# A modulation read as rows and an S5 state carried over token pairs: one change to a mixture-of-experts and state-space block in fp32

## The reference, cut to what matters

```python
cond = jax.nn.silu(c)                       # c: 1 x 1024
mod = cond @ ada_w[l] + ada_b[l]            # ada_w: 1024 x 6144
sh1, sc1, g1, sh2, sc2, g2 = jnp.split(mod, 6, axis=-1)
```

```
x[t] = a * x[t-1] + B u[t]          a = exp(lambda * step), complex, |a| < 1
y[t] = Re(C x[t]) + D * u[t]
```

## Time and profile before

| | us |
|---|---|
| median of the runs (3) | 3221.09 |
| the profiled execution | 3219.63 |
| its span in the trace | 3218.0 |
| TensorE busy | 2962.3 (92%) |
| VectorE busy | 1349.6 (42%) |
| ScalarE busy | 928.4 (29%) |

### The profile page before, as it was taken

The page is one execution under the profiler, slowest core; times in us unless marked ns, Lnnn a source line. Parts: engine busy times, 40 slices in busy tenths (PEclk is TensorE's granted clock), DMA queues, the critical chain, the costliest instruction groups (busy, mean ns, idle before and its releaser), DMA issues. The chain is left out here.

```text
span 3218.0 us, 46119 instructions
## 1 busy us (share of the span) xinstructions
PE 2962.3 (92%) x18349; PEld 2221.3 (69%) x18349; DVE 1349.6 (42%) x1820; ACT 928.4 (29%) x1160; POOL 68.1 (2%) x130
## 2 busy tenths in 40 slices
PE   8997899999999999999969999899799699999898
PEld 7886444334333333389858888899799587988897
DVE  1334311111111111154389756454544498645544
ACT  0122011111111111154222445344543222564443
POOL 3001000000000000010000000000100000000000
PEclk8958799999999999999989999999999899999899
DMA  6436499999999999985423433455565233525452
GB/s 215 144 117 233 175 418 418 417 418 418 418 418 418 417 418 418 413 243 191 128 67 105 154 112 123 151 178 169 150 219 168 73 94 104 168 98 163 155 184 79
DMA packets 343178, 737.74 MB, mean 229 GB/s; under 512 B 14200, under 2 KB 259504, under 8 KB 308224
## 3 DMA queue, kind: packets, MB, share of 16 engines
q1 hardware_dynamic: 338272, 726.71, 62.0%
q0 software_dynamic: 4768, 9.12, 1.3%
HBM read 734.73 MB, written 1.05 MB: 229 GB/s over the span
## 5 line engine op out<-in xcount | busy, mean ns | idle before, releaser
L476 PE MATMUL ps<-arena,ring 128*128 128x256 f32 x2304 | 520.3, 386 | 4.6 <-DVE arena L380 4.6
L1352 PE MATMUL ps<-u_upper,w_lower 128*128 128x256 f32 x1984 | 522.9, 284 | 0.6 <-DVEq L2191 0.5
L476 PEld LDWEIGHTS ps<-arena,ring 128*128 128x128 f32 x2304 | 440.7, 193 | 70.1 <-DVE arena L380 4.9
L1352 PE MATMUL ps<-u_upper,w_upper 128*128 128x256 f32 x1408 | 400.5, 284 | 3.5 <-DVE u_lower L1746 3.5
L1352 PE MATMUL ps<-u_lower,w_upper 128*128 128x256 f32 x1408 | 399.3, 284 | 0.0
L1740 DVE TENSOR_TENSOR w_lower<-ring,w_upper 128x2048 fp32r<-128x2048 f32 x128 | 293.3, 2292 | 215.9 <-ACT w_upper L1705 215.9
L1389 PE MATMUL ps<-arena 128*64 128x512 f32 x1632 | 365.4, 598 | 13.9 <-DMA arena<-in_exp_w_up 13.9
L1352 PEld LDWEIGHTS ps<-u_upper,w_lower 128*128 128x128 f32 x1984 | 367.7, 192 | 1.4 <-DVEq L2191 1.4
L1504 DVE TENSOR_SCALAR arena<-ps 128x512 f32<-128x512 f32 x34 | 23.5, 692 | 791.1 <-PE ps L1389 791.1
L1705 ACT ACTIVATE w_upper<-ring 128x2048 fp32r<-128x2048 f32 x128 | 244.7, 1912 | 195.8 <-PE ps L1352 195.7
L1389 PEld LDWEIGHTS ps<-arena 128*64 128x64 f32 x1632 | 110.2, 137 | 251.9 <-issue 197.6
(11 more groups left out here) (581 smaller groups left out, 3783.9 us busy)
## 6 DMA issues: line engine op xcount, KB each, us to landing
arena<-in_exp_w_up SPq DMA_DIRECT2D x204, 1024.0 KB, 20.2
ring<-in_exp_w_down SPq DMA_DIRECT2D x136, 1024.0 KB, 22.4
ring<-in_w_in SPq DMA_DIRECT2D x75, 1024.0 KB, 5.8
ring<-in_exp_w_up SPq DMA_DIRECT2D x68, 1024.0 KB, 24.1
ring<-in_ffn_w_gate SPq DMA_DIRECT2D x44, 1024.0 KB, 5.8
ring<-in_ffn_w_up SPq DMA_DIRECT2D x44, 1024.0 KB, 5.4
ring<-in_ffn_w_down SPq DMA_DIRECT2D x44, 1024.0 KB, 4.9
ring<-in_ada_w SPq DMA_DIRECT2D x24, 1024.0 KB, 5.2
```

What stands on the lines that cost most here:

```text
L476: ins = nc.tensor.matmul(bank(b, 2, TOK)[:, m, :], w[:, k, m * P:(m + 1) * P], rhs[:, k, :], start=(k == 0 and (part is None or (part == 0 ...
L1352: ins = nc.tensor.matmul(out_, w_ if w_is_lhs else x_, x_ if w_is_lhs else w_, start=start and n == 0, stop=stop and n == 2, skip_group_ch ...
```

## The change

**Modulation.** `ada_w` is read in 24 row slices of 128 x 2048, one DMA of 8 KB runs each. `mod_slice` has one column of `cond` as the stationary operand (128 x 1) and the slice as the moving one: four matmuls of 512 columns, which write to the partitions 0, 32, 64 and 96 of one bank. Eight slices give 2048 outputs, as rows. ScalarE copies four rows out of PSUM (`mod_rows_copy`), and `mod_turn` brings those that are wanted over the partitions there with 16 matmuls of one row by one column. `gate_spread` spreads a gate over the partitions with two matmuls of 512 columns. The 16 slices of the second half all stand in the first two rounds of the attention, eight to a round; the third round has only the 16 turns. The tiles of the gates in `gla_pe` and `lru_pe` are gone.

**S5.** The state is carried over pairs of tokens: `x[2c+1] = a^2 x[2c-1] + (aB) u[2c] + B u[2c+1]`. All 256 tokens of a group fit into one unit of 128 columns, so that there are 4 units and no `carry`. The inputs are 32 matmuls for each unit, two adding up in each place, with `u5` read at every other column. The outputs at the odd tokens come as before from C; those at the even ones from `(aC) x[2c-1]` and a direct term `CB u[2c]`: 72 matmuls for each unit. The matrices `aB` (`B_pair`), `aC` (`pair_C`) and `CB` (`direct`, 64 small matmuls) are new.

**The place of the parameters.** VectorE starts on them at once after the norm, beside the `u` products, and ScalarE takes over the copies of `u5` and of the transposed matrices. `s5_turn_pe` is called three times (C after the first `u` tile, B after the third, `B_pair` after the fourth).

```diff
-            for t in range(8):
-                load_tile(sp, T_ADA + t, 0, a["ada_w"][0, :, t * W:(t + 1) * W])
+            def ada_rows(T, c0):
+                for k in range(KT):
+                    load_slot(sp, T + k, 0, a["ada_w"][0, k * P:(k + 1) * P, c0:c0 + 2048])
+            ada_rows(T_ADA, 0)
...
+            ada_rows(T_ADA2, 2048)
+            ada_rows(T_ADA2 + KT, 4096)
...
+        def mod_slice(pe, T, b, k):
             landed(pe, T, 0)
+            for q in range(4):
+                ins = nc.tensor.matmul(bank(b, 512)[32 * q:32 * q + 1, :], small[:, 8 + k:9 + k],
+                                       ring[:, T % SLOTS, 512 * q:512 * q + 512], start=(k == 0), stop=(k == KT - 1),
+                                       skip_group_check=True)
             ins.then_inc(w_used, 1)
+        def mod_rows_copy(act, n, b, T):
+            multiplied(act, T + KT - 1, 0)
+            for q in range(4):
+                r = slice(32 * q, 32 * q + 1)
+                ins = nc.scalar.activation(mod_rows[r, n, :], bank(b, 512)[r, :], ACT.Copy)
+            ins.then_inc(sem("mod_rows"), 1)
+        def mod_turn(pe, b, n, q0, count):
+            for c in range(count):
+                q = q0 + c // 4
+                ins = nc.tensor.matmul(bank(b + c // 4, 4)[:, c % 4:c % 4 + 1],
+                                       mod_rows[32 * q:32 * q + 1, n, (c % 4) * P:(c % 4 + 1) * P],
+                                       one[32 * q:32 * q + 1, :], start=True, stop=True)
+            return ins
...
@@ attention_pe
-                for t in range(3 * r, min(3 * r + 3, 8)):
-                    mod_tile(pe, T_ADA2 + t, 7 if r < 2 else 3, 2 * t)
+                    pe.wait_ge(sem("mod_rows"), 3)
+                    mod_turn(pe, 0, 1, 2, 8)
+                    mod_turn(pe, 2, 2, 0, 8).then_inc(sem("mod_turned"), 1)
+                else:
+                    for k in range(KT):
+                        mod_slice(pe, T_ADA2 + KT * r + k, 7 - r, k)
...
@@ gla_pe, and the same in lru_pe
-            for t in range(4):
-                gate_tile(pe, T_ADA_G0 + t, 2 + t // 2, t % 2)
+            gate_spread(pe, 1, 0, 2, 3)
...
@@ u5_pe
             for n in range(4):
                 feature_tile(pe, L_U5 + n, r, n, uT, strip=strip if n == 0 else None)
+                if n == 0:
+                    pe.wait_ge(sem("s5_mats"), li * 3 + 1)
+                    s5_turn_pe(pe, C_nat)
+                if n == 2:
+                    pe.wait_ge(sem("s5_mats"), li * 3 + 2)
+                    pe.wait_ge(sem("s5_mats_ready"), li * 4 + 1)
+                    s5_turn_pe(pe, B_nat)
+            pe.wait_ge(sem("s5_mats"), li * 3 + 3)
+            pe.wait_ge(sem("s5_mats_ready"), li * 4 + 2)
+            s5_turn_pe(pe, B_pair)
+            pe.wait_ge(sem("s5_mats_ready"), li * 4 + 3)
+            s5_direct_pe(pe)
...
+        def s5_in_mm(pe, li, g):
             for o in range(4):
                 r = slice(32 * o, 32 * o + 32)
                 for v in range(2):
                     for q in range(2):
+                        T = 2 * g + q
+                        for e in range(2):
+                            ins = nc.tensor.matmul(bank(o, 2, 2, TC)[:, v, q, :], (pair_B, B_T)[e][v][r, T, :],
+                                                   parity(u5[r, T, :], e), start=(e == 0), stop=(e == 1),
+                                                   skip_group_check=True)
...
@@ s5_pe
+            for g in range(UNITS):
+                side_tile(pe, li, r, 4 * g)
+                side_tile(pe, li, r, 4 * g + 1)
+                if g + 1 < UNITS:
+                    pe.wait_ge(sem("s5_bu_read"), li * UNITS + g + 1)
+                    s5_in_mm(pe, li, g + 1)
+                    side_tile(pe, li, r, 4 * g + 2)
+                pe.wait_ge(sem("s5_states"), li * UNITS + g + 1)
+                if g == 0:
+                    pe.wait_ge(sem("s5_mats_ready"), li * 4 + 4)
+                s5_out_mm(pe, li, g)
+                if g + 1 < UNITS:
+                    side_tile(pe, li, r, 4 * g + 3)
+            side_tile(pe, li, r, 14)
             side_tile(pe, li, r, 15)
...
@@ s5_params_act
+            s5_u(act, r, 0)
+            s5_turned(act, li, 0, C_T)
+            s5_tables(act, li, 0)
+            s5_u(act, r, 1)
+            s5_u(act, r, 2)
+            s5_turned(act, li, 1, B_T)
+            s5_u(act, r, 3)
+            s5_turned(act, li, 2, pair_B)
+            act.wait_ge(sem("s5_turned"), li * 13 + 13)
+            nc.scalar.activation(direct, bank(4, 8, 32), ACT.Copy).then_inc(sem("s5_mats_ready"), 1)
...
@@ s5_act
             for n in range(15):
-                if n % 4 == 2 and n < 12:
-                    tables(n // 4 + 1)
+                if n in (1, 5, 9):
+                    s5_tables(act, li, n // 4 + 1)
                 side_read(act, li, r, n)
```

More of the change, by code:

```diff
@@ L731, in mod_pe @@
             pe.wait_ge(sem("cond_ready"), 1)
[L732 to L734 removed]
+            for k in range(KT):
+                mod_slice(pe, T_ADA + k, 0, k)
+                if k == 5:
                     pe.wait_ge(sem("consts"), 1)
@@ L1546, in build @@
         atab = [ffn_buf[:, 1024 * k:1024 * k + 1024].rearrange("p (o q t) -> p o q t", o=4, q=2) for k in range(2)]
-        carry, small_t = view(33344, 4, 4, 2), view(33376, 4, 4, 2)
+        direct = view(33344, 8, 32)
+        pair_mats = view(14336, 8, 4, P)
+        pair_B, pair_C = [pair_mats[:, :, v, :] for v in range(2)], [pair_mats[:, :, 2 + v, :] for v in range(2)]
         def layer_loads(pool, li):
@@ new lines, in s5_params_dve @@
+            t4 = [w.rearrange("p o q t -> p (o q t)").rearrange("p (a b c) -> p a b c", b=4, c=32) for w in work]
+            dve.wait_ge(sem("s5_mats_ready"), li * 4 + 1)
+            v.tensor_tensor(t4[0], blocks(C_T[0]), wide4(c_kr), ALU.mult)
+            v.tensor_tensor(t4[1], blocks(C_T[1]), wide4(c_ki), ALU.mult)
+            v.tensor_tensor(t4[2], blocks(C_T[1]), wide4(c_kr), ALU.mult)
+            v.tensor_tensor(t4[3], blocks(C_T[0]), wide4(c_ki), ALU.mult)
+            dve.drain()
+            v.tensor_tensor(blocks(pair_C[0]), t4[0], t4[1], ALU.add)
@@ L1878, in s5_params_act @@
+            v.tensor_tensor(blocks(pair_C[1]), t4[2], t4[3], ALU.subtract)
+            dve.drain()
+        B_pair = [w.rearrange("p o q t -> p (o q t)").rearrange("p (a b) -> p a b", b=32) for w in work[4:6]]
+        def s5_params_act(act, li, r):
             act.wait_ge(sem("s5_re"), li + 1)
@@ L1898, in s5_turn_pe, with s5_direct_pe @@
+                    ins = nc.tensor.transpose(bank(4 + k, 4, P)[:, q, :], src, ident[:])
                 ins.then_inc(sem("s5_turned"), 1)
-        NTC = TOK // TC
-        UNITS = 4 * NTC
+        def s5_direct_pe(pe):
+            for T in range(8):
+                for v in range(2):
+                    for o in range(4):
+                        j = slice(32 * o, 32 * o + 32)
+                        ins = nc.tensor.matmul(bank(4, 8, 32)[j, T, :], B_nat[v][:, 4 * T + o, :], C_T[v][:, T, j],
+                                               start=(v == 0), stop=(v == 1), skip_group_check=True)
+            ins.then_inc(sem("s5_turned"), 1)
@@ L2002, in s5_dve @@
-            angles(0, work[0])
-            for n in range(UNITS):
-                g, c = n // NTC, n % NTC
-                x, sums, parts = UNIT[n]
+                    T = 2 * g + q
+                    v.scalar_tensor_tensor(out=pairs(y5[:, T, :]), in0=pairs(u5[:, T, :]),
+                                           scalar=col(vec2, V2["s5_d"] + T),
+                                           in1=bank(4 + g % 2, 2, 2, TC)[:, q, :, :].rearrange("p e c -> p c e"),
+                                           op0=ALU.mult, op1=ALU.add)
```

295 lines of the change are left out of this document (137 added, 158 removed).

## The result

The changed kernel takes **3149.0 us** (median of 4 runs, 3147.9 to 3150.6) against 3221.6 for the kernel before on the same chip: a ratio of 0.977, 95% interval 0.976 to 0.979. Forecast were 3115, with a range of 3090 to 3155. All differences in time further down are between medians of different measurements; the kernel before had 3221.6, 3223.4, 3222.6 and 3225.2 in the four of them, so that less than about 4 us between two kernels says nothing. The profiled execution has a span of 3148.0 us; all that follows is from it. It is 70 us shorter than the span before: 43 went ahead of the experts, 28 in the two S5 branches.

What follows compares the result with a forecast made beforehand. Bounds by stage: TensorE and DMA near their limits first, the weights' transfer in the experts, TensorE and VectorE balanced in S5. 3219.6 - 40 (early part) - 64 (S5, both layers) = 3115.6, said as 3115; range 3090 to 3155.

Steps and rivals of the forecast that it cites:

- the early part: First modulation, attention and gates, ahead of the experts: -26.5 - 16.3 + 2.7 = -40 us.
- rival 1: First modulation and attention: column tiles of one column don't run side by side; early -6 instead of -40, 3150; chance 9%.
- rival 2: S5 loop: a new wait because VectorE or ScalarE is late, each layer 15 us, 3145; chance 8%.
- The one for `u` to projection: S5 branch: the stretch from the first `u` tile to the next projection takes 192 us, 32 less per layer.
- First modulation: Ahead of the first projection: slices of four column tiles, 1.7 us each at half clock; 26.5 us less (20 to 31).
- Attention: The three attention rounds: 44.9 us against 61.2, becoming transfer-bound; 16.3 less (10 to 20).
- Gates: Gate tiles up to the output projection: 1.3 us won, 4 lost to a lower clock without their cover; net +2.7.
- S5, the `u` stage: Ahead of the S5 loop: four `u` tiles at 6.91 us, transposes 6, `direct` 2.5, wait for `pair_B`'s copies 1.6.
- S5, outputs: S5 loop: 72 matmuls at 54 ns and a tail, 4.1 us a unit (before 1.95 for 32).
- strided read at half speed: S5 loop: a moving operand at every other column doubles 40 matmuls a unit, 3167; chance 5%.
- S5, inputs: S5 loop: 32 matmuls a unit take 6.3 us (5.6 to 6.9), from 2.8 us for 16.
- rival 3: S5 loops: longer quarter-tile blocks count as rest and TensorE's clock falls; 3420 at 0.50 throughout; chance 4%.

Runs made afterwards that it cites:

- in_contiguous: The kernel after, with the moving operand of the S5 inputs' block read as 128 neighbouring columns instead of every second one: 3147.0 us.
- side_direct_later: The kernel after, with the inputs' four row groups side by side and the direct term moved behind the first side tile: 3075.1 us, ratio 0.955.
- in_side_thrice: The kernel of side_direct_later, with the whole inputs' block, row groups side by side, done three times over: 3107.6 us.

## Why the prediction was right, and where it was not

**Mechanism and sign** were right but for one block, and the time lies within the range; 34 us of the forecast gain of 106 are missing. One term, the inputs, with the tiles right behind them, lost 37; the early part and the `u` stage were 3 and 4 us better than forecast, the outputs 4 worse. The total alone proves little: rival 1 was priced at 3150 and the first part of rival 2 at 3145, so it is the stages that speak for the forecast. Two of its signs of being wrong did come: input blocks over 7 us (8.0 to 10.2), and a granted clock under 0.9 in the loop (0.89 in both layers). The one for `u` to projection was missed too, 210.6 us instead of 192.

*First modulation*: -26.5 forecast, -30.8 measured (70.05 to 39.26). Side by side was right (1.9 us a slice, 1.7 forecast), and rival 1 is excluded by the single records and the rate; over the whole array a slice took 3.5. The slices landed somewhat earlier than my 31 us: the last two were multiplied by 28.9. The copies took 2.4 (2.6), the turns 3.6 (4.6), the norm 4.3.

*Attention*: 44.9 forecast, 44.8 measured (125.76 to 170.56), down to its course: transfer-bound behind six slices, last slice 29.8 us in.

*Gates*: +2.7 forecast, about +5 measured. From the third transposes to the output projection it is 60.6 us (58.8 before), the product 30.90 (27.79 before); a clock that fell because cover was gone was foreseen, its price of 4 us was near. In sum the early part gave 43 against 40.

*S5, the `u` stage*: 37.7 us forecast up to the first block, 35.7 measured. The three groups of turns took 1.91 us each (6 forecast for all). The cover of 2 us for `B_pair` held: the only wait is 0.90 for `pair_B`'s copies. In the loop no tile waits for a read, as the spare of 4 to 16 us had said; rival 2 did not come, nor did its strided read at half speed (in_contiguous). Taken away altogether, the cover by the `u` products is worth 51 us.

*S5, outputs*: 4.1 forecast, 4.6 measured. In the single records four matmuls start 7 ns apart and the next four 0.09 us behind them; where the tiles change from 128x32 to 32x32 or back it is 0.20 us. That is 0.11 more for each of the four changes inside a unit, the 0.5 that my sum lacked. The Trainium skill (TensorEngine Tiling (Array Packing), Tiling Modes, Key Properties) says that a change of tiling mode drains the engine. The trace agrees in so far as each of these changes costs something, about half the 0.2 us that I would have charged by that rule.

*S5, inputs*: **this term was mis-sized.** I scaled 2.8 us for 16 matmuls to 6.3 for 32 and took the clock as given. Measured were 8.0 to 10.2, some 11 us a layer too many, and the five tiles behind them cost 8 more (43 us, where five take 35.5 in side_direct_later): nearly 19 us a layer, 37 in all. The clock is nearly all of it. A block that kept it took 6.58; and a mean of 0.91 over 210.6 us is 38 us at half clock, which lose 19. It is rival 3's mechanism, in small: not the loop, only the four blocks and what is right behind them. I had argued against it with a clock of 0.92 and 0.91 in the branch before, "with all its waits in it". That said nothing of a block twice as long, and the clock after is 0.91 with no waits at all. The run with three blocks side by side shows that the order of the row groups decides. The run in halves shows fewer falls with shorter pieces; whether by their length or by their share of a longer stretch is open.

*The more useful miss*: I costed the block by its present order, "as four row groups overlap at their borders", and had in the same paragraph the outputs at 54 ns a matmul. Inputs at that rate, 32 x 0.06 = 2 us, would have shown that the order leaves two thirds of the block's time on the table, clock apart. The variant with the row groups side by side is 2% faster than the change.

## What to carry to other kernels

When matmuls use a part of the array, put the loop over the row or column groups innermost, so that neighbours use different parts: here it made a block 2.4 to 5 times shorter and kept the clock up for what stood behind it. It paid once TensorE set the loop; in the kernel before it only turned into waits. And when an edit makes a block of narrow matmuls longer, price the block and its neighbours at both clock levels.

## What the runs showed of the hardware

- TensorE's granted clock fell from its 2.4 to its 1.2 GHz level (1.00 to 0.50) within stretches in which it was busy 100% of the time: blocks of 32x128 tiles on one row group after another. It stayed full in 12 of 16 halves of 3.56 us; in the kernel after it was 0.64 to 0.78 over the whole blocks of the first layer and 0.73 to 0.81 over the single tiles behind them. With four row groups side by side, 5.7 to 6.2 us long, it was 1.00.
- Records of 32x128 tiles come 111 ns apart on one row group (3.56 us for 32), 33 ns apart on four (2.10 us for 64).
- Four column tiles with a single stationary column each run side by side (four records start within 20 ns, the next four 0.41 us behind): 0.89 us for 4 x 512 columns of fp32 at full clock, 1.9 at half; one after the other over the whole array, 3.5.
- A moving operand of fp32 that takes every second column costs nothing measurable (3149.0, against 3147.0 with neighbouring columns).
- Behind the 158th record after the wait ahead of the S5 loop TensorE stood still with no wait in the trace, in both layers of six kernels (0.4 to 2.9 us from start to start). The later blocks of 192 records in in_side_thrice (5.7 us each) have no such pause. The cause is open.
- After 9.2 us of matmuls at full clock and a wait of 2.88 us the clock fell just ahead of the next product (0.97 over the wait, 0.66 from 230 to 235 us).
